# A hybrid S5 and attention trunk on one core: turning the gated blocks of its feed-forward layers without TensorE

## The reference, cut to what matters

```
def swiglu(x, w_in, w_out):
    g, u = jnp.split(x @ w_in, 2, axis=-1)
    return (jax.nn.silu(g) * u) @ w_out
```

## Time and profile before

| | us |
|---|---|
| median of three runs | 972.12 |
| the profiled execution | 969.86 |
| its span (first to last instruction) | 967.7 |
| TensorE busy with matmuls | 955.9 (99%) |
| VectorE busy | 597.8 (62%) |
| ScalarE busy | 499.8 (52%) |
| GpSimd busy | 189.5 (20%) |
| share of time of the 16 DMA engines on the weights' queue | 54.5% |

### The profile page before, as it was taken

How to read it: one execution, slowest core, us unless ns; L and a number is a source line. 1 busy time by engine, 2 the same in 40 slices (tenths; PEclk the granted TensorE clock), 3 DMA queues, 4 the chain that set the end, 5 groups by cost and what they waited for, 6 DMA issues and landing times.

```text
span 967.7 us, 15102 instructions
## 1 busy us (share of the span) xinstructions
PE 955.9 (99%) x6110; PEld 790.2 (82%) x6110; DVE 597.8 (62%) x744; ACT 499.8 (52%) x711; POOL 189.5 (20%) x235
## 2 busy tenths in 40 slices
PE   9999999999999999999999999999999999999997
PEld 7888888788788888888888888888888888888886
DVE  5565779889765554656555555555557555656544
ACT  7554544576555454545544454554458454545441
POOL 4899999800000000000000000000060000000000
PEclk9999999999999999999999999999999999999999
DMA  9766555520455655565566666656651366555551
GB/s 347 269 184 197 181 174 174 175 69 5 142 187 193 194 178 194 184 208 183 166 198 196 193 177 196 191 177 195 188 182 45 111 198 193 186 187 192 179 169 43
DMA packets 47557, 169.35 MB, mean 175 GB/s; under 512 B 5505, under 2 KB 5505, under 8 KB 47489
## 3 DMA queue, kind: packets, MB, share of 16 engines
q1 hardware_dynamic: 47056, 167.79, 54.5%
q10 hardware_dynamic: 432, 0.61, 0.2%
HBM read 167.33 MB, written 1.05 MB: 174 GB/s over the span
## 4 chain that ended last, share of the span: by engine, by line
PE 88%; DVE 8%; issue 2%; ACT 1%; DMA 1%; SPq 0%; POOLq 0%; POOL 0%; DVEq 0%; ACTq 0%
PE ps L1252 85%; DVE w_lo L931 2%; PE ps L1257 2%; DVE scan L1158 1%; DVE tmp L1087 1%; PE ps L1284 1%; DMA raw<-in_in 1%; DVE rot_b L1165 1%; DVE rot_a L1145 1%; DVE rot_b L1147 1%; ACT w_hi L652 0%; DVE rot_in L1154 0%; DVE states L1172 0%; PE ps L1297 0%; ACT pr L881 0%
## 5 line engine op out<-in xcount | busy, mean ns | idle before, releaser
L931 DVE TENSOR_TENSOR w_lo<-raw,w_hi 128x1024 fp32r<-128x1024 f32 x311 | 399.7, 1289 | 307.0 <-ACT w_hi L652 305.7
L652 ACT ACTIVATE w_hi<-raw 128x1024 fp32r<-128x1024 f32 x311 | 328.4, 1059 | 305.9 <-PE ps L1252 303.2
L1252 PE MATMUL ps<-w_hi,x_hi 128*128 128x512 f32 x896 | 352.4, 393 | 0.9 <-DVE w_lo L931 0.6
L1252 PE MATMUL ps<-w_hi,x_lo 128*128 128x512 f32 x896 | 349.3, 390 | 0.0
L1252 PE MATMUL ps<-w_lo,x_hi 128*128 128x512 f32 x896 | 349.2, 390 | 0.0
L1252 PEld LDWEIGHTS ps<-w_hi,x_hi 128*128 128x128 f32 x896 | 168.4, 188 | 37.2 <-DVE w_lo L931 1.4
L1252 PEld LDWEIGHTS ps<-w_hi,x_lo 128*128 128x128 f32 x896 | 168.3, 188 | 35.2
L1252 PEld LDWEIGHTS ps<-w_lo,x_hi 128*128 128x128 f32 x896 | 168.5, 188 | 34.0
L1252 PE MATMUL ps<-w_hi,hid_hi 128*128 128x512 f32 x352 | 138.1, 392 | 1.0 <-DVE w_lo L931 1.0
L1252 PE MATMUL ps<-w_lo,hid_hi 128*128 128x512 f32 x352 | 137.2, 390 | 0.0
L1252 PE MATMUL ps<-w_hi,hid_lo 128*128 128x512 f32 x352 | 137.2, 390 | 0.0
(11 more groups left out here) (151 smaller groups left out, 599.6 us busy)
## 6 DMA issues: line engine op xcount, KB each, us to landing
raw<-in_in SPq DMA_DIRECT2D x175, 512.0 KB, 4.3
raw<-in_out SPq DMA_DIRECT2D x88, 512.0 KB, 3.4
raw<-in_glu SPq DMA_DIRECT2D x16, 512.0 KB, 4.3
raw<-in_k SPq DMA_DIRECT2D x8, 512.0 KB, 4.4
raw<-in_v SPq DMA_DIRECT2D x8, 512.0 KB, 4.1
raw<-in_q SPq DMA_DIRECT2D x8, 512.0 KB, 4.4
raw<-in_o SPq DMA_DIRECT2D x8, 512.0 KB, 4.0
xt<-in_xt SPq DMA_DIRECT2D x4, 256.0 KB, 5.6
```

What stands on the lines that cost most here:

```text
L652: act.activation(w_hi[:, gu % WS, :], raw[:, gu % RAW, :], ACT.Copy)\
L931: dve.tensor_tensor(w_lo[:, gu % WS, :], raw[:, gu % RAW, :], w_hi[:, gu % WS, :].bitcast(F32), ALU.subtract)\
L1252: return pe.matmul(o, w, x, start=start, stop=stop, skip_group_check=True)
```

## The change

A gated block is turned in two steps, one block at a time. VectorE transposes the 32 x 32 squares of the block in place, with one instruction over 128 x 512 elements. The squares then have to change places between groups of 32 partitions: 16 transfers per block (four source groups by four destination groups), each 32 partitions x 4 runs of 32 elements (128 bytes), 16 KB, from `prod` to `hid_lo`. SP issues them on the queue of the weights, after load number `MOVE_BEHIND` = 8 units past the step at which the block is gated, and it waits for the transpose (`hid_squares`) first. ScalarE then copies `hid_lo` to `hid_hi`, and VectorE subtracts in place in `hid_lo`; both now read SBUF where they read PSUM before. In an "in" phase block b - 2 is copied at step 1 of block b and subtracted at step 2; blocks 9 and 10 follow at steps 1/2 and 4/5 of the "out" phase. The product is stored with the two halves of 128 channels outermost. `turn_hidden` is gone from TensorE's program.

```
+Q = 32
+QS = P // Q
+SLOTS = 4
+MOVE_BEHIND = 8
+def gate_unit(p, b):
+    return (b + 1) * p.upb + (2 if p.n == 0 and b == 0 else 0)
 def high_behind(p, phases, b, j):
+    if p.name == "in" and b >= 2 and j == 1:
+        return [(p, b - 2)]
+    if p.name == "out" and b == 0 and j in (1, 4):
+        f = phases[p.n - 1]
+        return [(f, f.blocks - 2 + j // 4)]
 def low_behind(p, phases, b, j):
+    if p.name == "in" and b >= 2 and j == 2:
+        return [(p, b - 2)]
+    if p.name == "out" and b == 0 and j in (2, 5):
+        return [(f, f.blocks - 2 + j // 5)]
+        def tile_of(g, q):
+            return prod_of(g).rearrange("p i (t x) -> p t i x", x=P)[:, q]
+        def pieces(g, q, c):
+            return prod_of(g)[Q * q:Q * q + Q].rearrange("p t (a c x) -> p c (t a) x", a=2, x=Q)[:, c]
+        def places(b, q, c):
+            return hid_lo[Q * c:Q * c + Q, 2 * b:2 * b + 2, :].bitcast(F32)\
+                .rearrange("p i (t q x) -> p q (i t) x", t=TT, x=Q)[:, q]
 # SP
+            def move_hidden(p, b):
+                g = p.hid0 + b
+                sp.wait_ge(hid_squares, g + 1)
+                for q in range(QS):
+                    for c in range(QS):
+                        sp.dma_start(places(b, q, c), pieces(g, q, c)).then_inc(hid_moved[g % SLOTS], 16)
+            moves = {p.unit0 + gate_unit(p, b) + MOVE_BEHIND: (p, b)
+                     for p in phases if p.name == "in" for b in range(p.blocks)}
             for gu in range(10, len(units)):
                 load(gu)
+                if gu in moves:
+                    move_hidden(*moves[gu])
 # ScalarE
             def high_hidden(p, b):
-                act.wait_ge(hid_turned, p.hid0 + min(b // BATCH * BATCH + BATCH, p.blocks))
-                act.activation(halves(hid_hi[:, 2 * b:2 * b + 2, :].rearrange("p f x -> p (f x)")),
-                               turned_block(b), ACT.Copy).then_inc(hid_hi_done, 1)
+                act.wait_ge(hid_moved[g % SLOTS], 16 * QS * QS * (g // SLOTS + 1))
+                act.activation(hid_hi[:, 2 * b:2 * b + 2, :], hid_lo[:, 2 * b:2 * b + 2, :].bitcast(F32),
+                               ACT.Copy).then_inc(hid_hi_done, 1)
 # VectorE, in gated(p, b)
+                if p.name == "in":
+                    dve.wait_ge(drained, p.drained0 + TT * (b + 1))
+                    whole = prod_of(p.hid0 + b).rearrange("p t x -> p (t x)")
+                    dve.transpose(whole, whole).then_inc(hid_squares, 1)
             def low_hidden(p, b):
-                dve.wait_ge(hid_hi_done, p.hid0 + min(b // 2 * 2 + 2, p.blocks))
-                dve.tensor_tensor(halves(hid_lo[:, 2 * b:2 * b + 2, :].rearrange("p f x -> p (f x)")),
-                                  turned_block(b),
-                                  halves(hid_hi[:, 2 * b:2 * b + 2, :].rearrange("p f x -> p (f x)")
-                                         .bitcast(F32)), ALU.subtract).then_inc(hid_ready, 1)
+                dve.wait_ge(hid_hi_done, p.hid0 + b + 1)
+                part = hid_lo[:, 2 * b:2 * b + 2, :]
+                dve.tensor_tensor(part, part.bitcast(F32), hid_hi[:, 2 * b:2 * b + 2, :].bitcast(F32),
+                                  ALU.subtract).then_inc(hid_ready, 1)
 # TensorE
-            def turn_hidden(f, batch):
-                pe.wait_ge(drained, f.drained0 + TT * (batch[-1] + 1))
-                ...
-                for b in batch:
-                    for i in range(2):
-                        for q in range(TT):
-                            last = turn(KT + b % BATCH // 2 * 2, b % 2 * HB + (2 * i + q) * HP,
-                                        prod_of(b)[:, q, i * P:i * P + P])
-                    last.then_inc(hid_turned, 1)
-                        if j == 1:
-                            turn_hidden(*batch_behind(p, phases, b))
```

More of the change, by code:

```diff
@@ L67 @@
 FINAL = 12
-BATCH = 4
-BATCHES = (0, 4, 8)
+SLOTS = 4
+MOVE_BEHIND = 8
 TABLE_AT = (1, 3, 5, 7, 9, 11, 12, 13, 14, 15, 16, 17)
@@ L108, in follow_ups, with high_behind @@
     return [(phases[p.n - 1], phases[p.n - 1].blocks - 1, j)] if chained else []
[L111 to L115, removed]
-        f = phases[p.n - 1]
[L117 to L129, removed]
+def gate_unit(p, b):
+    return (b + 1) * p.upb + (2 if p.n == 0 and b == 0 else 0)
+def high_behind(p, phases, b, j):
+    if p.name == "in" and b >= 2 and j == 1:
+        return [(p, b - 2)]
+    if p.name == "out" and b == 0 and j in (1, 4):
+        f = phases[p.n - 1]
+        return [(f, f.blocks - 2 + j // 4)]
     return []
 def low_behind(p, phases, b, j):
[L135 to L140, removed]
+    if p.name == "in" and b >= 2 and j == 2:
[3 more added lines that the diff above has]
+        return [(f, f.blocks - 2 + j // 5)]
     return []
@@ L258, in w_columns, with prod_of @@
             return w2[:, :, :, PPT * d:PPT * d + PPT, :].rearrange("p r s g j -> p (r s) g j")
-        def prod_of(b):
-            i = b % BATCH
+        def prod_of(g):
+            i = g % SLOTS
             return prod[:, i] if i < 2 else prod2[:, i - 2]
+        def tile_of(g, q):
[5 more added lines that the diff above has]
+                .rearrange("p i (t q x) -> p q (i t) x", t=TT, x=Q)[:, q]
         def halves(a):
             return a.rearrange("p (b h x) -> p b h x", h=2, x=HP)
-        def turned_block(b):
-            at, col = KT + b % BATCH // 2 * 2, b % 2 * HB
-            return ps[:, at:at + 2, col:col + HB].rearrange("p h (b x) -> p b h x", x=HP)
         def z_place(d):
@@ L303, in trunk @@
         act_ready = sem("act_ready")
-        hid_turned = sem("hid_turned")
+        hid_squares = sem("hid_squares")
+        hid_moved = [sem(f"hid_moved{i}") for i in range(SLOTS)]
         hid_hi_done = sem("hid_hi_done")
@@ L965, in gated @@
                     if p.name == "in":
[L966 to L971, removed]
+                        g = p.hid0 + b
+                        if g >= SLOTS:
+                            dve.wait_ge(hid_moved[g % SLOTS], 16 * QS * QS * (g // SLOTS))
+                        dve.scalar_tensor_tensor(tile_of(g, q), halved(ps[:, bank(gb, q), HB:NB]),
+                                                 rs[:, q:q + 1], halved(act_out[:, q, :]),
                                                  ALU.mult, ALU.mult).then_inc(drained, 1)
@@ L1258, in turn @@
                 return last
-            def turn_hidden(f, batch):
-                if not batch:
-                    return
-                pe.wait_ge(drained, f.drained0 + TT * (batch[-1] + 1))
-                if f.hid0 + batch[0]:
-                    pe.wait_ge(hid_ready, f.hid0 + batch[0])
-                if f.n == 7 and batch[0] == 0:
-                    pe.wait_ge(kq_ready, 4)
-                for b in batch:
-                    for i in range(2):
-                        for q in range(TT):
-                            last = turn(KT + b % BATCH // 2 * 2, b % 2 * HB + (2 * i + q) * HP,
-                                        prod_of(b)[:, q, i * P:i * P + P])
-                    last.then_inc(hid_turned, 1)
             def turn_h(p, c):
```

## The result

The changed kernel takes 1036.41 us (median of four runs, 1035.4 to 1042.71) against 973.2 us for the kernel before beside it (972.08 to 974.7): a ratio of 1.066, 95% interval 1.062 to 1.071. It is 63 us slower. The prediction was 969.6 with a range of 961 to 978, so it was wrong in sign and in size. The profiled span went from 967.7 to 1033.7 us, 66.0 more.

The account below looks back on a forecast made before the run. TensorE was taken as the bound, except GpSimd's chain in the first fifth. Turns removed gain 11.6, layer 0 adds 9.1: 969.9 - 11.6 + 9.1 = 967.4 profiled, 972.1 - 2.5 = 969.6 us against the median; range 961 to 978.

Parts of the forecast that it names:

- What bounds the kernel, and the turns: TensorE bounds phases 3, 7 and 11; removing its transposes gains 3 x 3.86 = 11.6 us, layer 0's 3.9 us nothing.
- VectorE: Its 44 transposes of squares take 0.69 us each, hidden in phase 3, where 1.4 would be hidden too.
- SP and the transfers: 16 moves and 4 loads take SP 7.4 us of issues per block of 10.9 us.
- the lower row: The cheaper issue price for SP's moves, 0.37 us each with gap, taken because a move has 128 runs like a load.
- Cost zero: SP's extra issues and the moved blocks' landing add no time to the kernel.
- The bound from above, 13.8: SP's issues per block at the dearer price: 20 x 0.69 = 13.8 us.
- rival 3: SP or the DMA engines bound the "in" phases above 0.54 us per issue; 1032 us at 0.69; chance 0.13.
- A miss by 3 us would be taken up by the three units of lead: If a moved block reached ScalarE 3 us late, the lead in weight units would cover it, at no cost.
- The transfers themselves: Small packets take 2.7 us of each DMA engine per block; a move lands in about 2 us.
- GpSimd: In layer 0, subtraction from two SBUF inputs delays GpSimd's chain 6.4 us, order 1.7; `cp` ends 8.1 later, at 186.8.
- Rival 2: VectorE's transposes hold GpSimd up too: 6.4 us more, 976.0 us; chance 0.12.
- The clock: In layer 0, near 180 us, TensorE idles 11 us and its clock falls, costing 1.5 us (between 0 and 5.4).
- Rival 4: Moves come late, ScalarE waits at step 4 of each "out" phase: 1 to 3 us per phase, 975 us; chance 0.06.

Follow-up runs that it names:

- e1: The changed kernel with its 16 moves per block left out, squares read where they stand in `prod`: 964.77 us, ratio 0.992.
- e8: The changed kernel with blocks sent through HBM instead of moved, but layer 0's first pair keeping TensorE's turns: 960.01 us, ratio 0.989.
- e7: The changed kernel with the 16 moves replaced by one send to HBM and four fetches per block, everything computed: 963.33 us, ratio 0.992.
- e4: The kernel before plus one unread extra transfer, of eight shapes in turn, behind each of 24 weight loads of phase 7: 972.97 us.
- e11: The changed kernel with 12 moves per block issued by SP and four by ScalarE, everything computed: 962.9 us, ratio 0.993.
- e12: The changed kernel without moves, with phase 0's subtraction taking its first input from PSUM: 963.01 us, ratio 0.993.
- e9: The changed kernel with 14 of the 16 moves per block, values read in `prod`, moves waited for: 980.85 us, ratio 1.011.
- e5: The kernel before, turns kept, with the 16 moves per block added in phases 3, 7 and 11 into an unread buffer: 1004.05 us, ratio 1.032.

## Why the prediction was wrong, step by step

**What bounds the kernel, and the turns: right.** Phases 3, 7 and 11 gain 11.8 us in e1, where nothing else stands in the way, against 11.6 forecast; e8's span is 10.2 less with 1.4 lost in layer 0 (259.86 against 258.41 us at the same point of the "glu" phase). Layer 0's turns were worth nothing, as said: keeping them in e8, and leaving the rest of the change out there too, even gained 3.3 us over e7.

**VectorE: right.** The transpose takes 0.712 us (0.69 taken) and is hidden in phases 3, 7 and 11, or e1 would not gain the whole 3.9 us in each.

**SP and the transfers: the step that failed.** "16 x 0.37 + 4 x 0.37 = 7.4 us ... I take the lower row." Measured are 0.645 and 0.50, 12.4 by medians and 12.56 on the average of phase 3, against the 10.9 of a block; the term "Cost zero" was 72 us. The bound from above, 13.8, held it, and rival 3 had the right mechanism and the right point (0.54 us per issue); I gave it 0.13. That its price of 1032 comes so near 1036 is luck: it took a rate that is too slow (2.9 us above a block instead of 1.7) and a cover of 14 us a phase that was not there. With the measured rate its own sum is 4 x (18.5 - 14) = 18, and 972.1 - 11.6 + 18 is about 978. The reason I took the lower row was that "a move has 128 runs like a load": I sorted the rows by runs. But all those rows were transfers with HBM at one end, and e4 shows that for the move's shape the ends make the price. No row stood for both ends on chip, and between 0.33 and 0.65 I should not have concentrated the chance on one end. For the loads 0.37 was too low as well: back to back they take 0.43, and the start of the trace of before had that.

"A miss by 3 us would be taken up by the three units of lead" was the second error, independent of the first. A lead covers a delay once; a rate is paid per block. 11 blocks x (12.56 - 10.88) = 18.5 us in phase 3, against 18.2 measured beside e1. Nor was there the 14 us of cover per phase that rival 3 counted: TensorE did live on the lead at first, but ScalarE takes a moved block in the order of its queue, before the weights that it would round ahead, and at the end of the phase everything stood until the last move had landed. What is left of the cover is 2.2 us a phase, and the lower clock behind the stop takes 1.9 of it back.

The transfers themselves were oversized: I had 2.7 us of each DMA engine per block for the small packets. The share of 0.61 over a block of 12.56 us is 7.7 us, against 0.59 x 11.22 = 6.6 before, so by my estimate they took 1.1. The landing of 2.4 us was near the 2 taken.

The Trainium skill ("DMA: Bandwidth & Descriptors", Issuing engines are not separate DMA queues) says that starting DMAs from several engines only saves the time on the sequencer, "which is usually small relative to the DMA itself". Beside one move that holds (0.6 us against 2.4 to landing), but landings overlap and issues do not: e11 saved just that time for four moves per block and gained 74 us.

**GpSimd: right mechanism, size too large.** e1's `hid_lo` rises to 1.786 us beside GpSimd, and with a PSUM input (e12) it stays at 0.683 at most, so two on-chip inputs and a GpSimd read do exclude each other. But `cp` ends 3.8 us later than before, not 8.1, and e12 gives the subtraction 2.05 us of it, 0.19 for each of the eleven blocks where I took 0.58. The rest, 1.8, has the size of the 1.7 that I had for work that changes sides; no run tests that. Nor is it shown why the eleven add up to so little. I suppose that a VectorE instruction delayed here delays the next one, whose own collision then falls elsewhere, so that prices of rows do not add along a chain in which both engines are full. In the changed kernel itself the term never came up: TensorE was late and `cp` ended at 170.6 us.

**Rival 2: out.** GpSimd's two instructions of together 2.21 us ran at full speed (1.06 each alone, rows 7) beside a transpose in e1:

```profile
95.98 2.21 POOL L482 TENSOR_TENSOR tmp<-w,sm 128x512 f32<-128x512 f32 x2
...
96.67 0.71 DVE L999 STREAM_TRANSPOSE prod<-prod 128x512 f32<-128x512 f32 x1
```

In the stretch of 106 to 130 us the pairs with a transpose beside them take 3.07 us and the pairs without one 3.39. So the sentence of the Trainium skill that the prediction left open, on an instruction with one input from on-chip memory ("SBUF — State Buffer", Who interferes with whom) holds for the transpose.

**The clock: right in kind, the size near by luck.** In e1, by stretch, columns as in rows 10:

```profile
182.00:186.00 4.00, 1.01 (x6) 0.50 (x4) 1.55 (x2) 3.43 (x5) 2.79 (x11) 1.00 0.22 88
186.00:190.00 4.00, 4.00 (x11) 3.13 (x12) 3.97 (x5) 4.00 (x7) 1.54 (x3) 0.57 0.61 160
```

TensorE is busy for 1.01 of the four us before 186, and in the next four its granted clock is 0.57, mostly the 1.2 GHz level. The 48 matmuls take 12.79 us instead of 48 x 0.2267 = 10.9: 1.9, where I took 1.5. But I had expected some 11 us without work, and here there were about 3 in one piece. Of the 7.0 us that e1 loses before phase 3, 4.7 have come up by the end of phase 1; 2.3 more come up by the end of the "glu" phase, and which engine sets them was not tried.

**Rival 4** (moves only late) did not occur by itself: with 12 moves on SP and four on ScalarE the waits for moved blocks are 40.5 us in 18, and phases 3 and 4 take what they take without a move.

## What to carry to other kernels

Count the issues of every queue per unit of work, loads and additions together, and compare the sum with the bound's pace: below it an issue cost nothing here, above it each cost its full time for every unit. A lead takes off a part once, not per unit: 2 us a phase where a reader waited for the last of the additions (e9, and 16 moves), 6 where none did (e5). Before taking an issue's price from a row, ask whether source and destination are of the same kind as in the row; where no row has that, keep both ends alive in the chances too. When the queue is the bound, give a part of the issues to an engine that has time, or make fewer and larger transfers, and leave the old way where its cost is hidden.

## What the runs showed of the hardware that I had not expected

An issue with both ends in on-chip memory took SP 0.49 to 0.68 us, with HBM at one end 0.327 (a load, a send, and a 32 x 4 x 128-byte read alike), and a load right behind one of the former 0.58, right behind another load 0.43. A fetch from HBM in 16 pieces for each of 32 partitions took 0.636. VectorE's transpose of 32 x 32 squares took 0.712 us for 128 x 512 float32, near one plain pass (0.684), and did not hold GpSimd up.
